# An encoder layer on one core: memory attention in another order, and the down projection with tokens on the output partitions

## What is computed

```python
def mem_xattn(h, m, w_q, w_kv, w_o):              # 4 heads of 128, 256 memory tokens
    q = (h @ w_q).reshape(B, S, MEM_HEADS, MEM_HD) * (MEM_HD ** -0.5)
    k, v = jnp.split((m @ w_kv).reshape(B, M, 2 * MEM_HEADS, MEM_HD), 2, axis=2)
    p = jax.nn.softmax(jnp.einsum('bshd,bmhd->bhsm', q, k), axis=-1)
    o = jnp.einsum('bhsm,bmhd->bshd', p, v).reshape(B, S, MEM_HEADS * MEM_HD)
    return o @ w_o

def conv_ffn(h, w_up, conv_w, conv_b, w_down):    # w_down: (2816, 1024)
    ...
    return (jax.nn.silu(a) * u) @ w_down

x = x + mem_xattn(rms_norm(x, norm_mem_g[l]), rms_norm(mem, mem_norm_g[l]), w_mq[l], w_mkv[l], w_mo[l])
x = x + conv_ffn(rms_norm(x, norm_ffn_g[l]), w_up[l], conv_w[l], conv_b[l], w_down[l])
return rms_norm(x, final_norm_g)
```

## Time and profile before

| | us |
|---|---|
| median of 3 runs | 991.19 (989.63 to 991.42) |
| profiled execution | 991.44 |
| its span | 989.7 |
| PE busy | 969.3 (98%) |
| DVE, ACT, POOL busy | 574.1, 396.5, 34.5 |

### The profile page before, as it was taken

How to read it: one execution, slowest core, us unless ns; L and a number is a source line. 1 busy time by engine, 2 the same in 40 slices (tenths; PEclk the granted TensorE clock), 3 DMA queues, 4 the chain that set the end, 5 groups by cost and what they waited for, 6 DMA issues and landing times.

```text
span 989.7 us, 12244 instructions
## 1 busy us (share of the span) xinstructions
PE 969.3 (98%) x4803; PEld 810.9 (82%) x4803; DVE 574.1 (58%) x658; ACT 396.5 (40%) x433; POOL 34.5 (3%) x27
## 2 busy tenths in 40 slices
PE   6999999999999999999999989999999999999996
PEld 5899889777788888888888968888888888888885
DVE  4877555554548654466545547787677677632322
ACT  6363223333643652233433445544444444422221
POOL 1000000200000000000021004100000000000000
PEclk8999999999999999999999999999999999999998
DMA  7414212122123244323323214334333432233322
GB/s 248 147 49 128 66 62 86 47 92 66 41 64 107 75 142 117 87 80 106 127 85 128 64 64 119 94 88 123 87 85 100 112 85 72 87 90 113 89 58 85
DMA packets 141080, 93.24 MB, mean 94 GB/s; under 512 B 4502, under 2 KB 138998, under 8 KB 140918
## 3 DMA queue, kind: packets, MB, share of 16 engines
q1 hardware_dynamic: 141046, 92.75, 31.4%
HBM read 90.64 MB, written 2.10 MB: 94 GB/s over the span
## 4 chain that ended last, share of the span: by engine, by line
PE 95%; DVE 2%; ACT 1%; DMA 1%; SPq 1%; issue 0%; DVEq 0%; ACTq 0%
PE ps L483 80%; PE ps L806 4%; PE ps L590 2%; PE ps L527 2%; PE ps L582 1%; PE ps L820 1%; DMA raw<-in_w_in 1%; PE ps L836 1%; PE ps L627 1%; PE ps L533 1%; PE ps L541 1%; PE ps L596 1%; ACT wH L975 0%; DVE hgF L1298 0%; DVE hgG L1461 0%
## 5 line engine op out<-in xcount | busy, mean ns | idle before, releaser
L483 PE MATMUL ps<-hH,wH 128*128 128x512 f32 x784 | 310.2, 396 | 1.8 <-DVE hL L1305 1.8
L483 PE MATMUL ps<-hL,wH 128*128 128x512 f32 x784 | 306.8, 391 | 0.0
L483 PE MATMUL ps<-hH,wL 128*128 128x512 f32 x784 | 306.6, 391 | 0.0
L1298 DVE TENSOR_TENSOR wL<-raw,wH 128x2048 fp32r<-128x2048 f32 (+3 forms) x94 | 190.4, 2026 | 124.1 <-ACT wH L975 124.1
L975 ACT ACTIVATE wH<-raw 128x2048 fp32r<-128x2048 f32 (+3 forms) x94 | 159.7, 1699 | 222.8 <-PE ps L483 219.8
L483 PEld LDWEIGHTS ps<-hH,wH 128*128 128x128 f32 x784 | 148.2, 189 | 35.5 <-DVE wL L1298 2.5
L483 PEld LDWEIGHTS ps<-hH,wL 128*128 128x128 f32 x784 | 148.1, 189 | 31.1
L483 PEld LDWEIGHTS ps<-hL,wH 128*128 128x128 f32 x784 | 148.2, 189 | 30.4 <-issue 0.2
L483 PE MATMUL ps<-actH,wH 128*128 128x512 f32 x176 | 69.1, 393 | 0.0
L483 PE MATMUL ps<-actH,wL 128*128 128x512 f32 x176 | 68.6, 390 | 0.0
L483 PE MATMUL ps<-actL,wH 128*128 128x512 f32 x176 | 68.5, 389 | 0.0
(11 more groups left out here) (275 smaller groups left out, 1280.6 us busy)
## 6 DMA issues: line engine op xcount, KB each, us to landing
raw<-in_w_in SPq DMA_DIRECT2D x58, 512.0 KB, 4.1
raw<-in_w_up SPq DMA_DIRECT2D x44, 512.0 KB, 4.5
raw<-in_w_branch SPq DMA_DIRECT2D x24, 256.0 KB, 4.3
raw<-in_w_down SPq DMA_DIRECT2D x16, 384.0 KB, 3.2
raw<-in_w_down SPq DMA_DIRECT2D x16, 320.0 KB, 3.7
raw<-in_w_out SPq DMA_DIRECT2D x8, 512.0 KB, 4.0
raw<-in_w_mkv SPq DMA_DIRECT2D x8, 512.0 KB, 4.4
xtok<-in_x SPq DMA_DIRECT2D x4, 512.0 KB, 6.1
```

The source lines that it names most:

```text
L483: last = pe.matmul(out_ap, a, b, start=start and k + m == 0, stop=stop and m == 2 and k == len(terms) - 1)
L1298: q.sig(dve.tensor_tensor(out_ap, a, b, op), sem)
```

## The change

In the attention three engines get another order. ACT's `hi(Slot(N_MO + 1))` (slot 52) moves from ahead of the exponentials of head 3 to behind the copies of its transposes. DVE's `lo` of the same slot moves from ahead of `a_normed(3)` to behind the first two `a_lower`. TensorE computes the values of head 1 ahead of the transposes of head 2, and those of head 3 inside the first slot of the output projection, which now goes head by head.

The down projection becomes 11 slots of two row blocks (256 rows of w_down, all 1024 columns, rows of 4 KB). Tiles of actH and actL are loaded into the array, wH and wL stream; the output has tokens on its partitions and fills all 8 banks, two per tile of 128 tokens, summed over all slots. Each bank is first seeded with the residual, transposed by TensorE from xT (`seed`). In the last slot the tiles finish one after another, and each is normalised straight out of PSUM: ACT squares it with a sum along the row and takes the root, DVE takes the reciprocal and multiplies by it and by the gain, which a transfer has spread over all partitions (gainF). Output leaves in five pieces, the last two of 256 KB.

```diff
@@ PE, attention
             a_values(0)
+            a_values(1)
             a_transposes(2)
             mem_values(Slot(N_MV + 1), 1)
-            a_values(1)
             a_transposes(3)
             pe.wait_ge(taken, N_MO)
             a_values(2)
-            a_values(3)
...
-                    pe.wait_ge(a_ready, 2)
                     vh, vl = weights(n, KB, 256)
-                    for heads in (range(H - 1), (H - 1,)):
+                    for h in range(H):
+                        if h == 2:
+                            a_values(3)
+                        pe.wait_ge(a_ready, max(h + 1, 2))
                         for e, done in ((0, first_done), (1, slot_done)):
...
@@ PE, down projection
+            def seed(t):
+
+                for k in range(KD):
+                    b = (2 * t + 4 + k // 4) % 8
+                    pe.matmul(ps[:, b, P * (k % 4):P * (k % 4) + P], xT[:, k, P * t:P * t + P], ident[:, :],
+                              is_transpose=True, start=k % 4 == 0, stop=False, skip_group_check=True)
+
+            def down(j, tiles):
+
+                n = Slot(N_DN + j)
+                vh, vl = weights(n, 2, D)
+                for t in tiles:
+                    f = slice(P * t, P * t + P)
+                    for c in range(2):
+                        b = (2 * t + 4 + c) % 8
+                        g = slice(S * c, S * c + S)
+                        for k in range(2):
+                            ah, al = actH[:, 2 * j + k, f], actL[:, 2 * j + k, f]
+                            for m, (x, w) in enumerate(((ah, vh), (ah, vl), (al, vh))):
+                                last = pe.matmul(ps[:, b, :], x, w[:, k, g], start=False,
+                                                 stop=j == N_DNS - 1 and k == 1 and m == 2, skip_group_check=True)
+                        if j == N_DNS - 1:
+                            last.then_inc(o_new, 1)
+                return last
...
+            seed(0)
+            seed(1)
+            for j in range(N_DNS):
+                enter(Slot(N_DN + j), banks=False)
+                pe.wait_ge(f_ready, 2 * j + 2)
+                if j == 0:
+                    down(j, (0, 1))
+                    pe.wait_ge(taken, N_DN - 1)
+                    seed(3)
+                    pe.wait_ge(taken, N_DN)
+                    seed(2)
+                    last = down(j, (3, 2))
+                else:
+                    last = down(j, range(NT))
+                if j < N_DNS - 1:
+                    last.then_inc(slot_done, 1)
@@ ACT, end
+            for t in range(NT - 1):
+                act.wait_ge(o_new, 2 * t + 2)
+                do(osq[:, t, :], ps[:, bank(t, 0):bank(t, 0) + 2, :].rearrange("p b c -> p (b c)"), ACT.Square,
+                   accum_out=ostat[:, t, 0:1])
+                q.settle()
+                do(ostat[:, t, 2:3], ostat[:, t, 0:1], ACT.Sqrt, o_std, scale=1.0 / D, bias=eps[:, 0:1])
+            t = NT - 1
+            for c in range(2):
+                act.wait_ge(o_new, 2 * t + 1 + c)
+                do(osq[:, t, S * c:S * c + S], ps[:, bank(t, c), :], ACT.Square, o_sq if c == 0 else None,
+                   accum_out=ostat[:, t, c:c + 1])
...
@@ DVE, end
+                for c in range(2):
+                    b = (2 * t + 4 + c) % 8
+                    f = slice(S * c, S * c + S)
+                    stt(otok[:, t, f], ps[:, b, :], ostat[:, t, 3:4], gainF[:, f], ALU.mult, ALU.mult, o_fin)
@@ SP
+            sp.wait_ge(slot_done, N_MO)
+            sp.dma_start(gainF[:, :], final_norm_g.partition_broadcast(P)).then_inc(g_row, 16)
```

More of the change, by code:

```diff
@@ L369, in load_up, with load_down @@
                 load(n, *((v[:, h], wup[:, :, bass.ds(j * P + h * FF, P)]) for h in (0, 1)))
[L371 to L374, removed]
+            def load_down(n, j):
+                v = raw[n.s][:, :].rearrange("p (k c) -> p k c", k=2)
+                load(n, *((v[:, k, :], wdn[:, 2 * j + k, :]) for k in range(2)))
             xsrc = x[0].rearrange("(t p) d -> p t d", p=P)
@@ L883, in _ @@
                     enter(n)
-                    pe.wait_ge(a_ready, 2)
                     vh, vl = weights(n, KB, 256)
-                    for heads in (range(H - 1), (H - 1,)):
+                    for h in range(H):
+                        if h == 2:
+                            a_values(3)
+                        pe.wait_ge(a_ready, max(h + 1, 2))
                         for e, done in ((0, first_done), (1, slot_done)):
[L888 to L893, removed]
+                            f = slice(P * e, P * e + P)
+                            product(ps[:, 2 * n.s + e, :], [(vh[:, h, f], vl[:, h, f], moH[:, h, :], moL[:, h, :])],
+                                    done if h == H - 1 else None, start=h == 0, stop=h == H - 1)
                 else:
@@ L925, in _ @@
                     up(Slot(N_UP + 2 + k, i, 2))
[L928 to L951, removed]
-            pe.wait_ge(n_std, 2)
[L953 to L957, removed]
@@ L1252, in _ @@
                 q.leave(turns)
[L1254 to L1274, removed]
@@ L1276, in _ @@
-            act.wait_ge(f_ready, KF)
[L1277 to L1287, removed]
@@ L1288, in _, with bank @@
-            to_frames(Slot(KD - 1), 1)
-            act.wait_ge(o_ms, 1)
-            do(rstd[:, NT:2 * NT], ps[:, 0:NT, 0], ACT.Sqrt, o_std, scale=1.0 / D, bias=eps[:, 0:1])
+            act.wait_ge(f_ready, KF)
+            for j in range(2, N_DNS):
+                hi(Slot(N_DN + j))
+            def bank(t, c):
+                return (2 * t + 4 + c) % 8
+            for t in range(NT - 1):
+                act.wait_ge(o_new, 2 * t + 2)
[3 more added lines that the diff above has]
+                do(ostat[:, t, 2:3], ostat[:, t, 0:1], ACT.Sqrt, o_std, scale=1.0 / D, bias=eps[:, 0:1])
@@ L1293, in _ @@
+            t = NT - 1
[3 more added lines that the diff above has]
+                   accum_out=ostat[:, t, c:c + 1])
+            q.settle()
+            act.wait_ge(o_part, 1)
+            do(ostat[:, t, 2:3], ostat[:, t, 1:2], ACT.Sqrt, o_std, scale=1.0 / D, bias=ostat[:, t, 4:5])
         @block.vector
@@ L1770, in _ @@
             a_maximum(3)
-            lo(Slot(N_MO + 1), 4 * 256)
             a_normed(3)
             read_values(Slot(N_MV + 1), 256, (1,))
-            for h in range(H):
-                a_lower(h)
+            a_lower(0)
+            a_lower(1)
+            lo(Slot(N_MO + 1), 4 * 256)
+            a_lower(2)
+            a_lower(3)
             for c in range(4):
@@ L1834, in _ @@
                 q.leave(turns)
[L1836 to L1846, removed]
-                q.settle()
[L1848 to L1866, removed]
@@ L1867, in _ @@
-            dve.wait_ge(o_std, 1)
-            q.sig(dve.reciprocal(rstd[:, 0:NT], rstd[:, NT:2 * NT]))
-            q.settle()
-            dve.wait_ge(o_tok, KD)
-            for t in range(NT):
-                ts(otok[:, t, :], otok[:, t, :], rstd[:, t:t + 1], None, ALU.mult, sem=o_fin)
+            ffn_lower(Slot(N_DN - 1))
+            for j in range(2, N_DNS):
+                lo(Slot(N_DN + j))
+            dve.wait_ge(g_row, 16)
+            for t in range(NT):
+                if t == NT - 1:
+                    dve.wait_ge(o_sq, 1)
+                    ts(ostat[:, t, 4:5], ostat[:, t, 0:1], 1.0 / D, EPS, ALU.mult, ALU.add, sem=o_part)
+                dve.wait_ge(o_std, t + 1)
+                q.sig(dve.reciprocal(ostat[:, t, 3:4], ostat[:, t, 2:3]))
+                q.settle()
+                for c in range(2):
+                    b = (2 * t + 4 + c) % 8
+                    f = slice(S * c, S * c + S)
+                    stt(otok[:, t, f], ps[:, b, :], ostat[:, t, 3:4], gainF[:, f], ALU.mult, ALU.mult, o_fin)
```

30 lines of the change are left out of this document (15 added, 15 removed).

## The result

The changed kernel took 980.09 us (median of 4 runs, 978.62 to 982.24) against 990.84 (4 runs): ratio 0.9904, interval 0.9877 to 0.993 (estimated from all these runs; the quotient of the two medians is 0.9891). The forecast was 982.2, with a range of 980.4 to 985.4. The spans of the two profiled executions differ by 11.5 us (989.7 and 978.2). I cut them at landmarks that both programs have.

What follows compares the result with a forecast made beforehand. TensorE's own work was taken as the bound (95% of the chain). Attention 4.5 us plus tail 4.5 (5.0 gained, net of the down stage's 0.44) made 9.0: 991.44 to 982.4, or 982.2 against the median; range 980.4 to 985.4.

Steps and rivals of the forecast that it cites:

- The stall of head 3: Attention: ACT's exponentials stand 5 us late behind slot 52's conversion; the new order gains 4.5 us, 2.9 of it the stall.
- the half clock behind the stall: Attention: transposes and values after the stall ran at 1.2 GHz, losing 1.06 + 0.65 us, counted in the gain.
- the ordering round it: Attention: named with the half clock as the rest of the 4.5 us gain beyond the 2.9 us stall; no separate size.
- a_ready 2: Attention: DVE gives it at 586.5, wanted by TensorE at 587.2, so 0.7 us to spare.
- Head 3: Output projection: the only tight wait; 1.35 us to moL, 6 matmuls cover 1.37; charged 0.1 us.
- The load of gainF: Added 512 KB load: waits for slot_done 51, falls where DMA engines carry 0 to 3 GB/s.
- Down projection: Same 528 matmuls at the same pace, conversions and loads hidden; the stage gets 0.44 us longer.
- The seeds: Down projection: 32 seeds replace 28 transposes of back(), 4 x 0.11 = +0.44 us.
- The rival with the bank changes: Down stage: 88 changes cancel the gain at 0.10 us each, or lower the clock; chance 0.05 for both.
- The end: Last matmul readable to end of execution: 6.15 us instead of 11.12, so 5.0 gained.
- the landing of the last 256 KB: Tail: the last output piece takes 2.9 us, like a 256 KB load; bounds 2.6 and 4.6.
- the product of three operands out of PSUM: Tail: DVE's products taken at 0.75 us each, from a nearest case of 0.69; above 1 us would refute.

Runs made afterwards that it cites:

- the down part alone: The changed kernel with the attention orders of the kernel before, so only the down projection and end are changed; ratio 0.995 to before.
- the attention part alone: The kernel before with only the attention orders of the change, down projection and end as before; ratio 0.9965 to before.

## Why the prediction was right, point by point

- **The stall of head 3.** Right in place, cause and cure: ACT's exponentials behind a conversion that waited for another slot's end. Putting that one conversion (wH on ACT, wL on DVE) back brings the stall back, and more of it. 4.5 us were forecast, 4.22 measured against this profile of before.
- **What was wrong in it.** I counted the half clock behind the stall as a sure part of the gain. It is there in the profile of before, and not in that of the down part alone, with the same stall. So the edit is worth 2.7 us in the one case and 4.2 in the other; the interval of the attention part alone, 2.0 to 5.1 us, holds both. And I named "the ordering round it" as a part of the gain: it costs 0.35 us. My own terms left it no room: stall 2.9 and half clock 1.06 + 0.65 are 4.6, and that is what ACT's and DVE's queues alone give (46.02 - 41.43).
- **Waits of the new order.** a_ready 2 and slot 52 in time, as worked out. Head 3 was forecast to cost 0.1 us and cost 0.29. The 1.35 us were right (1.36), the cover was not: the first of the 6 matmuls starts before the end that the profile gives head 3's values (590.12), so the matmul behind them was due at 591.12 + 0.23 = 591.35, 1.23 and not 1.37 us behind that end. moL came at 591.48, 0.13 too late, TensorE started 0.06 behind it, and the next start took 0.10 more than the usual 0.23. The load of gainF did not fall where I put it, into the calm of the earlier trace rows: it was issued at 588.13, next to slot 54's load, in a stretch with 196 GB/s, and nothing waited for it.
- **Down projection.** Forecast +0.44, measured +0.27 from row sums to T, all of it in the stage (123.44 against 123.15). The seeds cost what I took, 3.50 us for 32 against 3.08 for the 28 transposes; the form and the changes of bank cost nothing, as the rows of the 256-column form and of the seeded matmuls had said (504 matmuls in 114.30 us, 0.2268 each). The rival with the bank changes is refuted at twice their number: granted clock 1.00 throughout. The Trainium skill (TensorE: Matmul & The Clock Gate, "A second HAM failure mode: psum-queue depth-cycling") puts the swings of its kernel down to small idles of TensorE between groups of matmuls. This stage has no such idles, so its rule isn't contradicted here; going round the banks alone doesn't bring them.
- **The end.** Forecast 6.15, measured 5.08. Up to the end of the products the terms held (T+2.66, forecast T+2.8); the product of three operands out of PSUM, which I said the trace lacked, stood in the trace of before at 0.745 us (last section). The mis-sized one is the landing of the last 256 KB: 2.0 us, not the 2.9 of a 256 KB load of wMO. That load was the wrong neighbour for this store. The Trainium skill's formula (DMA: Bandwidth & Descriptors, "Anatomy of one DMA — SWDGE (gpsimd) path"), which is for transfers issued from GpSimd while these go out from SP, gives an estimate of 2.6 for it, nearer but also long; for 512 KB it gives 3.2, and the pieces here landed in 2.6.
- **The total.** 9.0 forecast. By pieces against this profile of before 4.22 - 0.27 + 6.04 = 9.99; with the stall at full clock it would be 8.5. The medians differ by 10.75 us; the spans by 1.51 us more than the pieces account for, which is the first row of the table, and the ratio's interval (7 to 12 us) covers all of these. Three sets of runs of the changed kernel give 0.9904, 0.9919 and 0.9894. That the measured total came this close is in part luck: the half clock behind the stall (1.5 us) and the clock in the first 300 us (up to 4 us) change from one execution to the next, and the forecast took one profile's values for them.

## What to carry to other kernels

When TensorE waits, follow the chain to the queue in which the late instruction stood, and look what that queue's head was waiting for: in the attention, moving one conversion that waits for another slot out of the way of the softmax gave the gain (with one swap on ACT that wasn't tried alone), and reordering the waiting engine gave none. Let as many tiles of the last stage as possible finish under the matmuls of the next, with the result on the partitions on which it is written out; in this kernel the last transfer's landing then set the end, and having the output ready 0.66 us sooner gave nothing. And cut two profiles at common landmarks before crediting a difference in span to an edit.

## What was not expected of the hardware

- The same program's time goes with its mean granted clock. Of 23 runs of the kernel before in one set, six took 991.75 to 992.37 us with 0.988, and five 985.8 to 987.3 with 0.997; in the two later sets (22 runs) none had 0.997. The kernel before has one profile only. Over the profiles of all kernels the clock differs in the first 25 us, from 250 to 300 us and behind the stall: a stall of 2.9 us was followed by 1.2 GHz in the profile of before, one of 2.8 us by 2.4 GHz in that of the down part alone.
- The stores landed faster than the loads of their size: 256 KB in 2.0 us against 2.9 (w_mo), 512 KB in 2.6 against 3.7 (w_down in the changed kernel). That the direction is the cause isn't shown. The loads go out in pairs, and w_mo moves in rows of 1 KB, the last stores in rows of 2 KB; four stores of 512 KB issued 0.7 us apart, in the kernel before, took 2.6 to 4.6 us as well. Two stores of 256 KB issued 0.4 us apart took 2.0 and 2.3, two issued at once from two queues 2.5 and 2.7.
- A product of three operands costs DVE the same out of PSUM (second row, 746 ns) as out of SBUF (first row, 752). The groups of the changed kernel, and then the line of the kernel before that had this price out of PSUM already:

```profile
L1294 DVE SCALAR_TENSOR_TENSOR cu<-zu,par,cu 128x512 f32<-128x512 f32 x44 | 33.1, 752 | 27.6 <-ACT cu L980 24.6 <-DVE cu L1294 1.5
...
L1294 DVE SCALAR_TENSOR_TENSOR otok<-ps,ostat,gainF 128x512 f32<-128x512 f32 x8 | 5.6, 746 | 0.1
```

```profile
L1305 DVE SCALAR_TENSOR_TENSOR hL<-ps,par,hH x8: 745/745/747, 14.9 to 20.7; 128x512 fp32r<-128x512 f32 x8
```
